# A hand-ordered TensorE queue: side products of a recurrence moved beside other full-array products

## What is computed

```
def step(S, inp):
    r_t, w_t, k_t, v_t, kk_t, a_t = inp
    sa = jnp.einsum("bhvk,bhk->bhv", S, kk_t)
    S = (S * w_t[:, :, None, :]
         - sa[..., None] * (kk_t * a_t)[:, :, None, :]
         + v_t[..., None] * k_t[:, :, None, :])
    return S, jnp.einsum("bhvk,bhk->bhv", S, r_t)
```

## Time and profile before

| what | value |
|---|---|
| median of 3 runs | 2391.15 us (2391.08 to 2391.42) |
| profiled execution, its own time | 2391.0 us |
| its span in the trace | 2389.0 us |
| PE busy in the span | 99% |
| the loop, about 1555 to 2044 us | 32 turns |
| length of a steady turn | 15.83 (g = 0), 15.86 (g = 1), 15.01 (g = 2), 15.83 us (g = 3) |
| granted TensorE clock | 0.999 |

### The profile page before, as it was taken

The page is one execution under the profiler, slowest core; times in us unless marked ns, Lnnn a source line. Parts: engine busy times, 40 slices in busy tenths (PEclk is TensorE's granted clock), DMA queues, the critical chain, the costliest instruction groups (busy, mean ns, idle before and its releaser), DMA issues.

```text
span 2389.0 us, 54476 instructions
## 1 busy us (share of the span) xinstructions
PE 2361.2 (99%) x24052; PEld 2061.3 (86%) x24052; DVE 1530.5 (64%) x2964; ACT 559.3 (23%) x1289; POOL 418.2 (18%) x483
## 2 busy tenths in 40 slices
PE   8999999999999999999999999999999999999999
PEld 8999888899999998889999888488888889556558
DVE  7886674488778766744888887255555554147652
ACT  2101030111011010301111111245555554132341
POOL 1111000112011110001223320234444440100000
PEclk9999999999999999999999999999999999999999
DMA  7555544445545554545454321000000001212112
GB/s 279 188 179 192 188 182 148 168 162 201 198 166 190 182 194 177 179 156 178 176 194 160 109 85 71 1 3 4 3 3 3 3 4 38 89 53 88 53 53 71
DMA packets 40427, 285.03 MB, mean 119 GB/s; under 512 B 4544, under 2 KB 5744, under 8 KB 6272
## 3 DMA queue, kind: packets, MB, share of 16 engines
q1 hardware_dynamic: 36000, 252.83, 29.4%
q0 software_dynamic: 4192, 28.72, 3.3%
HBM read 280.48 MB, written 1.05 MB: 118 GB/s over the span
## 4 chain that ended last, share of the span: by engine, by line
PE 95%; DVE 3%; ACT 1%; issue 0%; DMA 0%; POOL 0%; SPq 0%; DVEq 0%; ACTq 0%; POOLq 0%
PE psum L696 27%; PE psum L1039 21%; PE psum L1100 12%; PE psum L1208 6%; PE psum L714 5%; PE psum L1338 3%; PE psum L1327 3%; PE psum L1340 2%; PE psum L1287 1%; PE psum L1427 1%; PE psum L1010 1%; PE psum L1274 1%; PE psum L1399 1%; PE psum L1411 1%; PE psum L1423 1%; PE psum L1355 1%
## 5 line engine op out<-in xcount | busy, mean ns | idle before, releaser
L696 PE MATMUL psum<-arena,ring 128*128 128x256 f32 (+1 forms) x2864 | 675.2, 395 | 8.8 <-ACT arena L1735 8.5
L696 PEld LDWEIGHTS psum<-arena,ring 128*128 128x128 f32 x2864 | 541.8, 190 | 130.3 <-issue 57.0
L1039 PE MATMUL psum<-arena 128*128 128x128 f32 x2560 | 325.0, 275 | 0.0
L1039 PEld LDWEIGHTS psum<-arena 128*128 128x128 f32 x2560 | 305.1, 192 | 0.0
L1039 PE MATMUL psum<-arena,ring 128*128 128x128 f32 x1920 | 253.6, 275 | 0.0
L1039 PEld LDWEIGHTS psum<-arena,ring 128*128 128x128 f32 x1920 | 233.9, 192 | 0.2
L2348 DVE TENSOR_TENSOR arena<-ring 128x1024 f32<-128x1024 f32 x136 | 171.1, 1258 | 39.1 <-PE psum L1100 34.8
L1100 PE MATMUL psum<-arena 128*128 128x128 f32 x1408 | 184.6, 275 | 0.0
L1100 PEld LDWEIGHTS psum<-arena 128*128 128x128 f32 x1408 | 170.7, 192 | 0.0
L2370 DVE SCALAR_TENSOR_TENSOR arena<-arena 128x256 f32<-128x256 f32 x336 | 164.1, 530 | 5.1
L1338 PE MATMUL psum<-arena 64*64 64x64 f32 x2560 | 158.6, 223 | 2.8 <-DVE arena L2763 2.8
(11 more groups left out here) (343 smaller groups left out, 3411.5 us busy)
## 6 DMA issues: line engine op xcount, KB each, us to landing
ring<-in_weights SPq DMA_DIRECT2D x238, 1024.0 KB, 4.8
arena<-in_ada POOLq DMA_DIRECT2D x24, 1024.0 KB, 5.4
arena<-in_const POOLq DMA_DIRECT2D x1, 1312.0 KB, 6.9
arena<-in_x SPq DMA_DIRECT2D x1, 1024.0 KB, 4.8
ring<-in_weights SPq DMA_DIRECT2D x2, 512.0 KB, 7.2
arena<-in_ctx POOLq DMA_DIRECT2D x1, 1024.0 KB, 6.2
arena<-in_lora POOLq DMA_DIRECT2D x1, 1024.0 KB, 5.2
out<-arena SPq DMA_DIRECT2D x8, 128.0 KB, 1.9
```

What stands on the lines that cost most here:

```text
L696: mm = self.nc.tensor.matmul(out, self.ring[:, slot % RING, i * P:(i + 1) * P], rhs, start=(kc == 0), stop=(kc == len(moving) - 1))
L1039: mm = nc.tensor.matmul(bank[:, n * P:(n + 1) * P], left[:, kind, pair, :], right[:, pair, :], start=(n == 0 and pair == 0), stop=(n == la ...
```

## The change

In TensorE's queue the middle side products go from behind `lower_product(q+1,1)` to directly behind `turned_v(q)`, and the end ones from behind `next_inverse(q+1,2)` to directly ahead of it, behind `out_and_state(k+1)`. On ScalarE, `take_gates("w",1)` of turn 0 goes from side_middle to directly behind `take_turned_v`. All products, banks and their order stay.

```
                 turned_bk(q)
                 turned_v(q)
+                side(q, "middle")
                 lower_product(q, 4)
                 if k >= 0:
                     out_and_state(k)
                 next_inverse(q, 4)
                 if ahead:
                     lower_product(q + 1, 1)
-                side(q, "middle")
                 if k >= 0:
                     state_product(k + 1)
...
                 if k >= 0:
                     out_and_state(k + 1)
+                side(q, "end")
                 if ahead:
                     next_inverse(q + 1, 2)
-                side(q, "end")
...
             def side_middle(q):
                 pair, g = divmod(q, GROUPS)
-                if q == 0:
-                    take_gates("w", 1)
                 if g == 1 and pair + 1 < PAIRS:
                     exponentials(pair + 1, 1)
...
                 take_turned_bk(q)
                 take_turned_v(q)
+                if q == 0:
+                    take_gates("w", 1)
                 if k >= 0:
                     take_o(k)
```

## The result

| | median of 5 runs | lowest to highest |
|---|---|---|
| before, same chip | 2391.3 us | 2391.08 to 2391.68 |
| changed | 2404.45 us | 2399.03 to 2404.56 |

Ratio 1.0049, 95% interval 1.0034 to 1.0063: slower by 0.5%. 2406.0 was predicted. The profiled execution took 2404.56 us.

A forecast was written before the change was run, and what follows sets the result against it. TensorE, busy 99% of the span, was taken to bound the loop by its order. Terms 3.3 + 0.6 + 5.8 + 1.5 + 8.7 + 0.8 - 0.3 - 5.4 = +15.0 on 2391.0 gave 2406.0 us, its own range 2401 to 2411.

The forecast's parts named there:

- The bank wait and the lost cover: Plain middle turn: product waits for ScalarE to empty its bank, +1.35; old place's stretch only 0.80 shorter: +0.55 us.
- The saved changes of form: TensorE: each end product saves 0.20 us between weight forms, 27 make 5.4; for middle products the wait covers the saving.
- ScalarE late in g = 0: take_gates queues behind the copy of next_inverse, so the middle product's bank empties late: +1.45 in six turns, 8.7 us.
- ScalarE late in g = 1: take_gates queues behind the copy of next_inverse, so bonus waits for its bank: +0.96 in six turns, 5.8 us.
- Turn 1: A table load lies on ScalarE's late chain and part of it shows already; estimated at +1.5 us.
- the 5% rival, VectorE beside GpSimd: VectorE operations with two SBUF inputs stretch while GpSimd works: 0.3 us in 22 turns, +6.6 more, 2412.6 us; 5%.
- one regular wait worth naming: In turns without a middle product, lower_product(q,5) waits for ScalarE's copy of level 4: stretch 2.36 us, not 2.17.
- Turn 31: No lower_product(q+1,1) there; the move gives up less cover but adds the full block ahead: about +0.8 us.
- Only the bank wait counts: Rival: ScalarE catches up, so g = 0 and g = 1 behave as in the trace; +7.3, 2398.3 us; 12%.
- The changes of form decide: Rival: no wait shows on TensorE, 11.6 us saved, 2379.4 us; 5%.
- The two cancel: Rival: waits are half the sum, an early wait making later ones vanish; result within 0.2% of before; 4%.

The follow-up runs named there:

- the last experiment: From the changed kernel with ScalarE's gates first: VectorE takes the middle product directly behind mask_lower(q,4), mask_stack(q,1) going behind update_state; 2389.86 us.

## Why the prediction held, point by point

The direction, the mechanism and the size were right: 2406.0 against 2404.45. That the sum comes within 2 us is in part luck, because misses cancel: turns 1, 2 and 31 cost 3.5 us more than forecast, and g = 1, turn 4 and the single turns 3, 27, 29 and 30 cost 3.2 less. Without the clock's fall in turn 1, which the forecast did not have, the median would have come out lower, as the run of 2399.03 us suggests. Per group of turns (the changed loop minus the one before, in us):

| term | forecast | measured |
|---|---|---|
| g = 3, turns 7 to 23: 5 x (0.55 - 0.20) | +1.75 | 5 x 0.31 = +1.6 |
| turns 3, 27, 29, 30 | +0.55 | -0.1 |
| g = 1, turns 5 to 25: 6 x (0.96 - 0.20) | +4.6 | 6 x 0.50 = +3.0 |
| g = 0, turns 8 to 24: 5 x (1.45 - 0.20) | +6.25 | 5 x 1.22 = +6.1 |
| turn 4 | +1.25 | +0.3 |
| g = 2, turns 6 to 26: 6 x -0.20 | -1.2 | 6 x -0.24 = -1.4 |
| turn 0 | -0.5 | -0.5 |
| turn 1 | +1.5 | +3.3 |
| turn 2 | 0 | +0.9 |
| turn 31 | +0.8 | +1.6 |
| loop (the parts are rounded) | +15.0 | +14.6 |

The span grew by 1.1 less than the loop, outside of it. 0.6 lie ahead of lower_product(0,3), where no edit acts. 0.5 lie right behind turn 31, where the next state_product waits 1.39 instead of 1.87 us; behind the very last out_and_state the two traces have the same length.

**The bank wait and the lost cover**: right. The plain turn was forecast at 16.2 and took 16.14. VectorE's share was 0.27 in the forecast and 0.20 in the last experiment. The part that was off is the wait of the second mask for side_middle, 0.09 in my sum. VectorE's rows in turn 11 of the changed kernel have it at 1739.57 - (1738.80 + 0.74) = 0.03:

```profile
1738.80 0.74 DVE L2725 SCALAR_TENSOR_TENSOR arena<-arena,psum 128x512 f32<-128x512 f32 x1
1739.57 0.42 DVE L2763 TENSOR_TENSOR arena<-psum,arena 128x256 f32<-128x256 f32 x1
```

**The saved changes of form**: right at the end (0.19 for 0.20). For the middle the forecast was that the wait covers all of it. With the block behind lower_product(q,4) a change shows again, at 0.15. The Trainium skill (TensorEngine Tiling (Array Packing), section Tiling Modes, key properties) says that changing the mode drains TensorE; the trace agrees for 128 x 64 behind 64 x 64, with that 0.15.

**ScalarE late in g = 0**: right to 0.03 in turns 8 to 24 (1.22 against 1.25). In turn 4 it was mis-sized: I took all six turns alike, but turn 4 has no table load of its own, and pays +0.3 like a plain turn.

**ScalarE late in g = 1**: right as a mechanism, 0.26 a turn too large. take_gates starts 1698.32 - 1697.52 = 0.80 behind first_gram, where I had 0.92 (read off turn 27, whose copy started later), and the stretch to solve is 2.51, not 2.63.

```profile
1698.32 1.26 ACT L1912 ACTIVATE arena<-psum,arena 128x512 f32<-128x512 f32 x2
```

**Turn 1**: the estimate of +1.5 took the table load as a plain delay. The wait grew to 2.15 and the clock fell behind it. With a wait of 0.72, in the kernel with the early table load, neither the fall nor the +3.3 is there. That a long wait brings a fall every time is not shown, and other rows speak against it. The state_product behind turn 31 waits 1.87 both with the end alone moved and in the kernel before, and the stretch behind that wait ran at half clock in the first (shown first) and at full clock in the second:

```profile
2042.96 0.34 PEld L1399 LDWEIGHTS psum<-arena,ring 64*64 64x64 f32 x8 [1.87 <-issue]
...
2043.45:2046.87 3.42, 3.42 (x4) 1.38 (x5) 0.29 (x1) 0.00 (x0) 0.00 (x0) 0.50 0.00 0
```

```profile
2046.32 0.34 PEld L1399 LDWEIGHTS psum<-arena,ring 64*64 64x64 f32 x8 [1.87 <-issue]
...
2046.83:2050.24 3.41, 3.41 (x8) 1.32 (x8) 0.29 (x1) 0.00 (x0) 0.00 (x0) 1.00 0.00 0
```

**Turn 2**, and the 5% rival, VectorE beside GpSimd. In turn 2 one VectorE operation took 1.58 us beside a GpSimd that is busy throughout, where it took 0.69 before (from 1589.19):

```profile
1591.34 1.58 DVE L2756 TENSOR_TENSOR arena<-arena 128x512 f32<-128x512 f32 x1
```

But this is not the only turn where it happens, and it is not new. In all six g = 2 turns from 6 to 26 the same operation takes 1.3 us, before as well as in the changed kernel, and TensorE waits for the mask queued behind it: 0.36 before, 0.31 in the changed kernel. Turn 10 of the kernel before:

```profile
1711.76 1.33 DVE L2756 TENSOR_TENSOR arena<-arena 128x512 f32<-128x512 f32 x1
...
1715.49 0.20 PEld L1338 LDWEIGHTS psum<-arena 64*64 64x64 f32 x4 [0.36 <-DVE arena L2763]
```

So the prediction's reading that there is one regular wait worth naming missed a second one. It changed the forecast little, since the whole change leaves most of it in place (0.30 and 0.24 us of the turn), but it is why either move alone shortens a g = 2 turn by more than its change of form. The rival's extra cost came in turn 2 alone (+0.9), not in 22 turns. That GpSimd is the cause is an inference from the overlap; that turn 2 is 13.54 again where turn 1 is on time is shown.

**Turn 31**: forecast from the middle's move alone (+0.8). The end product's cover of ScalarE's copy in turn 30 was overlooked; with the end alone moved the turn takes 11.34, 0.73 more than before, and leaving that product in place gives turn 31 all of it back, at the price of 0.20 in turn 30. **Turn 27**: the trace of before had an irregular 0.5 in it already (15.05 long, where 15.83 less the 1.25 of an end product is 14.58), so little was added.

**The rivals.** Only the bank wait counts: false, as ScalarE carries 11.6 us of the loop. The changes of form decide: false, though with ScalarE on time and the middle left alone the end's move is worth 7.3, some 5 of it by changes of form (27 times 0.19). The two cancel: false.

## What to carry to other kernels

On an engine that is busy all the time, a block's place is worth what it covers, not only what it costs: moving the side products ahead bared two copies and one bank that had been hidden behind them. Moving a product earlier on one queue makes its consumer late unless that consumer's queue moves with it; here the order of ScalarE's operations, with one table loaded in idle time, turned half of the change from a gain of 1 us into one of 8. Before such a move, follow the engine that must deliver next for a whole turn, and treat first and last turns by themselves: turns 1 and 31, two of 32, carried 4.8 of the 14.6 us.

## What the runs showed of the hardware

- One wait of 2.15 us on TensorE was followed by 3.41 us at a granted clock of 0.51, and the turn lost 3.5 us in all against a run whose wait was 0.72. Waits of 1.39 (turn 8) were followed by a clock of 1.00.
- The length of a wait alone does not tell whether the clock falls. Behind a wait of 1.87 us it fell in one trace (only the end products moved) and stayed at 1.00 in that of the kernel before. One later wait (ahead of L1587 in the kernel before, 3.63 to 3.66 us) is in every trace; the clock fell around it in eight and not in two. From the very last out_and_state on, the span was 1.5 us longer with such a fall of 3.41 us than without one (321.95 in the kernel before, 320.46 with all moves and ScalarE's gates first).
- A VectorE operation with two SBUF inputs (L2756) took 1.58 or 1.33 instead of 0.69 us in stretches where GpSimd was at work. That GpSimd is the cause is inferred from the overlap.
